# A gated layer's output projection, split by heads between the last group of heads and what follows it

## What is computed

```
def gated_delta_net(h, w_in, conv_w, a_log, dt_bias, norm_w, w_out):
    proj = h @ w_in
    ...
    o = chunk_gated_delta_rule(q, k, v, g, beta)
    o = rms_norm_2(o, norm_w) * jax.nn.silu(z.reshape(B, T, GDN_V_HEADS, GDN_HEAD_DIM))
    return o.reshape(B, T, GDN_V_W) @ w_out
...
        x = x + rms_norm_2(m, norm_mix_post[layer])
        h = rms_norm_2(x, norm_ffn_pre[layer])
        x = x + rms_norm_2(swiglu_2(h, ffn_w_gate[layer], ffn_w_up[layer], ffn_w_down[layer]),
                         norm_ffn_post[layer])
```

## Time and profile before

| | |
|---|---|
| median of 3 runs | 2587.55 us (2573.05 to 2587.69) |
| the profiled execution | span of 2583.7 us from the first to the last instruction |
| TensorE matmul busy, share of that span | 2399.0 us, 93% |
| VectorE, ScalarE, GpSimd | 61%, 45%, 29% |
| mean granted TensorE clock | 0.954 of full |
| the last group of heads, until its last chunk output | from 2222.5 to 2300.9 us |
| the output projection | from 2316.3 to 2364.2 us |

### The profile page before, as it was taken

One profiled execution on the slowest core, in us unless ns is written; L12 is line 12 of the kernel. 1 busy time (PEld: TensorE's weight loads), 2 busy tenths in 40 slices (PEclk: granted clock), 3 DMA queues, 4 the chain that ended last, 5 costly groups with the idle time before them and its releaser, 6 DMA issues. The chain is left out here.

```text
span 2583.7 us, 54823 instructions
## 1 busy us (share of the span) xinstructions
PE 2399.0 (93%) x21962; PEld 2304.5 (89%) x21962; DVE 1588.3 (61%) x2781; ACT 1171.5 (45%) x1907; POOL 739.6 (29%) x653
## 2 busy tenths in 40 slices
PE   7999798999999998999999988989988998879998
PEld 7999687999889998999899987889977888868998
DVE  3779796666524674766566688556675545335665
ACT  3534564443445664434444456444344434524343
POOL 1230496000186554000000078520024454510000
PEclk9999799999999999999999999999998988969999
DMA  4575200555455442555255543245531221203552
GB/s 166 193 200 181 73 1 17 172 185 179 138 174 169 126 136 92 172 185 180 90 187 179 166 140 137 97 142 181 185 116 59 75 79 64 92 2 130 196 185 91
DMA packets 103295, 344.48 MB, mean 133 GB/s; under 512 B 16336, under 2 KB 22000, under 8 KB 102592
## 3 DMA queue, kind: packets, MB, share of 16 engines
q1 hardware_dynamic: 102560, 340.66, 40.1%
q0 software_dynamic: 544, 1.12, 0.3%
HBM read 340.56 MB, written 1.16 MB: 132 GB/s over the span
## 5 line engine op out<-in xcount | busy, mean ns | idle before, releaser
L163 PE MATMUL ps<-h_high,hi 128*128 128x256 f32 x3320 | 977.8, 295 | 48.4 <-DVE h_low L327 29.1
L164 PE MATMUL ps<-h_low,hi 128*128 128x256 f32 x3320 | 954.6, 288 | 0.0
L165 PE MATMUL ps<-h_high,lo 128*128 128x256 f32 x3320 | 953.8, 287 | 0.0
L101 ACT ACTIVATE hi<-raw 128x1024 fp32r<-128x1024 f32 x623 | 648.1, 1052 | 385.2 <-PE ps L165 384.4
L163 PEld LDWEIGHTS ps<-h_high,hi 128*128 128x128 f32 x3320 | 652.0, 196 | 68.2 <-DVE h_low L327 34.2
L123 DVE TENSOR_TENSOR lo<-raw,hi 128x1024 fp32r<-128x1024 f32 x440 | 532.9, 1227 | 231.6 <-ACT hi L101 231.0
L164 PEld LDWEIGHTS ps<-h_low,hi 128*128 128x128 f32 x3320 | 652.8, 197 | 1.3 <-issue 0.6
L165 PEld LDWEIGHTS ps<-h_high,lo 128*128 128x128 f32 x3320 | 652.2, 196 | 0.0
L140 POOL TENSOR_TENSOR lo<-raw,hi 128x512 fp32r<-128x512 f32 x354 | 456.9, 1316 | 316.6 <-ACT hi L101 316.5
L164 PE MATMUL ps<-hidden_low,hi 128*128 128x256 f32 x1056 | 298.7, 283 | 0.0
L163 PE MATMUL ps<-hidden_high,hi 128*128 128x256 f32 x1056 | 296.7, 281 | 1.8 <-DVE lo L123 1.4
(11 more groups left out here) (456 smaller groups left out, 3610.8 us busy)
## 6 DMA issues: line engine op xcount, KB each, us to landing
raw<-in_weights SPq DMA_DIRECT2D x623, 512.0 KB, 3.4
at_bias<-bias_group SPq DMA_DIRECT2D x64, 64.0 KB, 2.7
s_bn<-in_s_bn SPq DMA_DIRECT2D x4, 512.0 KB, 4.7
consts<-in_consts SPq DMA_DIRECT2D x1, 1506.5 KB, 8.8
x<-in_x SPq DMA_DIRECT2D x1, 1024.0 KB, 4.9
s_cT<-in_s_b SPq DMA_DIRECT2D x1, 1024.0 KB, 7.4
s_cw<-in_s_c SPq DMA_DIRECT2D x1, 1024.0 KB, 10.5
s_cT<-s_rows POOLq DMA_DIRECT2D x16, 64.0 KB, 8.0
```

The source lines that it names most:

```text
L101: act.activation(k.hi[:, item % CUT, :], k.raw[:, item % RAW, :], ACT.Copy).then_inc(k.item_rounded, 1)
L163: pe.matmul(out, wh, xh, start=start, stop=False, **more)
L164: pe.matmul(out, wh, xl, start=False, stop=False, **more)
L165: return pe.matmul(out, wl, xh, start=False, stop=stop, **more)
```

## The change

`gdn_out` is dropped and its 128 products move into `gdn_heads`, which now runs with the feed-forward part and the last norm in one Block.

- The 128 products are cut into six parts by heads and columns. Parts 0 and 1 (heads 0 to 7, 64 products) are chained behind the 32 gate products as fill of the last group, which so has 96. Parts 2 and 3 (heads 8 to 11, 32 products) stand around the last group's closing norm: 6 before its sums, 10 between sums and rows, 16 after the rows. Parts 4 and 5 (heads 12 to 15, 32 products) follow.
- Heads 0 to 11 get their high part on ScalarE (`out_high`) and their low part on VectorE (`out_low`) within the last group, two heads after each of levels 1 to 4 and two at two of the chunk steps. GpSimd takes no low parts of heads any more. The pairs lie in the hidden buffers of the feed-forward part, in two new buffers of four tiles, and in the buffers of the layer's input, for which `part_free` waits.
- Columns 0 to 3 of heads 0 to 7 are added up in banks 4 and 5 and copied out (`kept`, two copies of 128 x 512 on VectorE, before its copies of `u`); later VectorE adds them into banks 0 and 1. The results end in banks 0, 1, 4 and 5, and the feed-forward part's gate and up products go to banks 2 and 3.
- All the output projection's weight items are rounded on ScalarE and cut on GpSimd (`cut_halves`); before, VectorE cut them. Weights are stored in the order of the parts.

```
+OUT_PARTS = [(range(0, 8), range(0, 4)), (range(0, 8), range(4, 8)), (range(8, 12), range(4, 8)), (range(8, 12), range(0, 4)),
+             (range(12, 16), range(0, 4)), (range(12, 16), range(4, 8))]
...
+    def part_free(engine, h):
+        if 6 <= h < 14:
+            engine.wait_ge(k.item_used, first + n_proj)
+        elif h >= 14:
+            engine.wait_ge(k.item_used, first + n_proj + 5)
...
+        def out_products(part):
+            heads, cols = OUT_PARTS[part]
...
+            if part == 0:
+                pe.wait_ge(g.read, n_proj)
+            for i, h in enumerate(heads):
+                pe.wait_ge(k.low_done.s, b_low + h + 1)
+                for c, n in enumerate(cols):
+                    if part == 1 and i == 0 and c % 2 == 0:
+                        pe.wait_ge(k.norm_out.s, b_kept + c // 2 + 1)
+                    pair, j = part_of(h)
+                    out = out_at(n + 4) if part == 0 else out_at(n)
...
+                    mm = product(pe, out, w.tile(n_proj * ITEM + at), pair_tile(pair, j), start=opening, stop=last and part in (0, 4, 5),
+                                 skip_group_check=True)
...
+            if hg == NG - 1:
+                fill = itertools.chain(fill, first_out_products())
...
+        fill = more_out_products()
+        some(fill, 6)
         head_sums(NG - 1, iter(()))
+        some(fill, 10)
         head_rows(NG - 1)
+        for _ in fill:
+            pass
+        for part in range(4, 6):
+            for _ in out_products(part):
+                pass
...
             if hg:
                 head_squares(hg - 1)
+            if not more:
+                out_high(0, 2)
             rounded(F, F + 1)
...
-                if more or l < 5:
-                    rounded(F + l - 1, F + l)
+                rounded(F + l - 1, F + l)
                 if hg and l == 4:
                     head_roots(hg - 1)
+                if not more and l < 5:
+                    out_high(2 * l - 2, 2 * l)
...
+                if not more and n in (1, 2):
+                    out_high(6 + 2 * n, 8 + 2 * n)
+                rounded(F + 7 + n, F + 8 + n)
...
         head_squares(NG - 1)
         head_roots(NG - 1)
+        rounded(F + 11, F + 15)
+        out_high(GH - HG, GH)
+        rounded(F + 15, F + 19)
...
+                if not more and l < 5:
+                    out_low(2 * l - 2, 2 * l)
+            if not more:
+                dve.wait_ge(k.item_used, first + n_proj + 4)
+                for b in range(2):
+                    dve.tensor_copy(kept[...], k.ps[:, 4 + b, :]).then_inc(k.norm_out.s, 1)
...
+                elif n in (2, 3):
+                    out_low(4 + 2 * n, 6 + 2 * n)
...
+        out_low(GH - HG, GH)
+        for b in range(2):
...
+            dve.tensor_tensor(k.ps[:, b, :], k.ps[:, b, :], kept[...], ALU.add).then_inc(k.out_done.s, 1)
...
-                if more or l < 6:
-                    cut(F + l - 2, F + l - 1)
+                cut(F + l - 2, F + l - 1)
...
+        cut(F + 9, F + 19)
...
+    k.result_banks, k.gate_banks = (0, 1, 4, 5), (2, 3)
```

More of the change, by code:

```diff
@@ L12 @@
+import itertools
 import math
@@ L417, in norm @@
         return Parts(k, src, pair, kt, gain_col, dst, slot)
[L420 to L457, removed]
 def swiglu(k, src, prep, side=None):
@@ L510, in gate_up @@
                     for j in range(KT):
-                        mm = product(pe, k.ps[:, 4 + b % 2, half * T:(half + 1) * T], w.tile((at + half) * ITEM + j),
+                        mm = product(pe, k.ps[:, gates[b % 2], half * T:(half + 1) * T], w.tile((at + half) * ITEM + j),
                                      pair_tile(src, j), start=(j == 0), stop=(j == KT - 1))
@@ L2545, in gdn_heads @@
     order = gdn_order()
-    first, n_out = k.used, len(order)
+    first, n_proj = k.used, len(order)
+    n_all = n_proj + GH * KT // ITEM
     z = sb("gdn_z", [P, 2 * HG, T])
@@ L2678, in _ @@
         sp.dma_start(par[:, 1, :], k.ins["gdn_dt_bias"].broadcast_to([P, GH])).then_inc(k.side_here.s, 16)
-        loads(k, sp, first, n_out)
+        loads(k, sp, first, n_all)
     @block.tensor
@@ L2723, in head_rows, with first_out_products, more_out_products @@
                     mm.then_inc(g.hw, 1)
+        def out_products(part):
+            heads, cols = OUT_PARTS[part]
+            at = sum(len(a) * len(b) for a, b in OUT_PARTS[:part])
+            if part == 0:
[7 more added lines that the diff above has]
+                    out = out_at(n + 4) if part == 0 else out_at(n)
+                    opening = part in (0, 1, 3) and i == 0 and c % 2 == 0
+                    last = i == len(heads) - 1
+                    mm = product(pe, out, w.tile(n_proj * ITEM + at), pair_tile(pair, j), start=opening, stop=last and part in (0, 4, 5),
+                                 skip_group_check=True)
+                    at += 1
+                    if part >= 4 and last and c == 1:
+                        mm.then_inc(k.result_done.s, 1)
+                    if at % ITEM == 0:
+                        mm.then_inc(k.item_used, 1)
+                    yield
+        def first_out_products():
+            for part in range(2):
+                yield from out_products(part)
+        def more_out_products():
+            for part in range(2, 4):
+                yield from out_products(part)
         prep.sums_before(pe)
@@ L3086, in head_variance, with out_low @@
             ins.then_inc(g.hv, 1)
+        def out_low(a, b):
+            for h in range(a, b):
+                pair, j = part_of(h)
+                dve.wait_ge(k.cut_round.s, b_high + h + 1)
+                dve.tensor_tensor(pair[1][:, j, :], v[:, h, :], pair[0][:, j, :].bitcast(F32), ALU.subtract).then_inc(k.low_done.s, 1)
         def head_inverse(hg):
@@ L3266, in _ @@
                     pool.tensor_tensor(op, op, z_of(hg - 1)[:, 2 * b:2 * b + 2, :], ALU.mult).then_inc(g.ho, 1)
-            if more:
-                cut(F + 5, F + 7)
+            cut(F + 5, F + 7)
             for n in (1, 2):
@@ L3272, in _ @@
                 pool.tensor_tensor(Sd[:, :, :], S[:, n % 2, :, :], spread(rx[:, :, end - 1:end], 2, P), ALU.mult).then_inc(g.sd, 1)
-                if more:
-                    cut(F + 6 + n, F + 7 + n)
+                cut(F + 6 + n, F + 7 + n)
             if more:
                 cut(F + 9, F + 12)
+        cut(F + 9, F + 19)
     A.n += 5
     k.side_here.n += 48
-    k.used += n_out
-    k.late = None
+    k.used += n_all
+    k.late = first + n_all - 1
+    k.result = [(k.out_done.s, b_added + 1), (k.out_done.s, b_added + 2), (k.result_done.s, b_res + 2), (k.item_used, first + n_all)]
+    for signal, n in ((k.mul_done, 2), (k.cut_round, GH), (k.low_done, GH), (k.norm_out, 2), (k.result_done, 2), (k.out_done, 2)):
+        signal.n += n
+    k.result_banks, k.gate_banks = (0, 1, 4, 5), (2, 3)
 def build(nc, ins, x_in, out, plan, n_items):
@@ L3333, in build @@
         k.act_done = counted("scalar_part_done")
-        k.norm_out = counted("norm_tile")
+        k.norm_out = counted("tile_written_by_vector")
         k.cut_round = counted("high_part")
@@ L3537, in gdn_items @@
 def gdn_items(inp):
-    w = inp["gdn_w_in_2"][0]
-    return np.concatenate([by_output(w[:, :6 * D])[gdn_order()], by_output(inp["gdn_w_out_2"][0])])
+    w, out = inp["gdn_w_in_2"][0], tiles(inp["gdn_w_out_2"][0])
+    out = np.concatenate([out[list(heads)][:, list(cols)].reshape(-1, P, P) for heads, cols in OUT_PARTS])
+    return np.concatenate([by_output(w[:, :6 * D])[gdn_order()], as_items(out)])
 def gdn_ba(inp):
```

49 lines of the change are left out of this document (35 added, 14 removed).

## The result

The changed kernel takes 2559.93 us, the median of four runs (2551.97, 2559.49, 2560.37 and 2576.32); the kernel before, with a fourth run added to the three shown ahead, 2583.05. The ratio is 0.9909 with a 95% interval of 0.9884 to 0.9935: faster by 23.1 us, 0.9%. The forecast of 2557.0 is 2.9 us off and the range holds it, but part of that agreement is luck: the saving was put at 30.5 us, 7.4 us too high, and the median of before came out 4.5 us lower than the one it was taken from, which hides most of that.

A forecast was written before the change was run, and what follows sets the result against it. TensorE, 93% busy, bounds the program, and engine-to-engine chains bound the last group and closing norm; 141.75 - 80.9 (group) - 30.3 (behind it) = 30.5 us saved, so 2587.55 - 30.5 = 2557 us, range 2544 to 2573.

The forecast's parts named there:

- The frame: From group 3's first key product to the feed-forward part's first sum of squares: 141.75 us replaced, 30.5 us saved.
- 3.9 us "around the span": Whole run: time of the profiled execution outside its span of 2583.7 us, together the median of 2587.55.
- Group 3 until level 3: Last group's start: TensorE's order unchanged, 24.4 us from the old trace plus 0.8 us.
- The +0.8: Ahead of level 2's copies on ScalarE: two high parts at 0.4 us each, all on the path.
- From level 3 to the end of the group: Group 3 to its last output: group 2's 57.1 us less 1.4 us of square sums.
- VectorE's and ScalarE's additions in the group: Group 3: at most 11.7 us more on VectorE and 13.1 us on ScalarE, costed at nothing.
- Behind the group: Last output to first feed-forward sum: 30.3 us, against 63.3 before.
- The fifth rival: Closing norm's chain as exposed as before: 39.9 us behind the group, 9.6 more, 2567 us; chance 0.04.
- The first, slots without free room: Last group's levels: group 85 to 95 us, 15 to 25 us saved, 2563 to 2573 us; chance 0.24.
- The second, that the clock stays up: Group 3: under 5 us at half clock, some 6 us more back and 2 behind, 2549 us; chance 0.14.
- The third, shared ports: VectorE's low parts and GpSimd's cuts wait for each other: 11 us less saved, 2568 us; chance 0.10.
- The fourth, queues that wait for each other: In-order queues in group and tail: slower than before, 2617 us at 6 us for each place; chance 0.06.

The follow-up runs named there:

- the repetition: The changed kernel run again unaltered, beside the kernel before: median 2563.2 us, ratio 0.9888.
- both edits: Changed kernel with four last-group level 2 products moved into the wait for ScalarE's copies and the last gate read at level 2's end: 2553.12 us, 0.9866 of before.
- the four after it: Both edits plus four products moved in groups 1 and 2 (2545.29, again 2548.54 us), or splits at later levels in group 3 (2551.69) or all groups (2540.68).

## Why the prediction held, and where its steps did not

**The frame.** Right: what follows the stretch takes 219.5 us in every trace, what precedes it differs by the clock of a stage with the same code, and the saving on the stretch (23.0 and 27.7 us) is about that of the medians (23.1 and 25.6). The 3.9 us "around the span" were not that: the changed kernel's profiled execution has 1.8. The rest was the distance between one execution and the median.

**Group 3 until level 3.** The term that was mis-sized is the one that took 24.4 us from the old trace "until level 3", plus 0.8. It measured 29.4 and 28.3 us in the changed kernel, for 25.2. The +0.8 was right in size (0.62 measured). What the term left out is that the old 24.4 us stood at full clock, and that the same order with a longer wait need not. With four products in the wait, level 3 comes at 23.6 to 23.7 us in each of the six traces of group 3 that have them there. Without them and with the wait of 1.9 us it comes at 28.2 to 29.4 in five of six, and at 25.0 in the sixth, the run without products of the output in the group. With the old wait of 1.27 us it comes at 24.4 in both traces. So it is shown that the loss is half clock and that the moved products keep it away; that the 0.62 us of longer wait brought it is possible, and not shown. The trace of before had the warning in it: in groups 1 and 2, which I took as the measured case of "this very order", level 3 comes at 30.9 and 29.7 us. I took the second half from group 2 and the first from group 3's own trace, where it was 5.3 us shorter.

**From level 3 to the end of the group.** 55.7 forecast, 58.2 measured. 1.05 us of that is the wait of the first output product for the last gate result, which the prediction didn't name though the diff shows the wait (`g.read`): shown by moving the read. The other 1.4 us go with the clock: from level 3 on the changed kernel has 14.0 us at half clock, and the piece of group 2 that was the model had 9.5. In the repetition, with 9.8, this part takes 56.4 us.

**VectorE's and ScalarE's additions in the group.** Cost at nothing: nothing speaks against it; no wait for a low part is in the group's list. VectorE was busy there for 34.0 us, forecast at most 36.8.

**Behind the group.** 30.3 forecast, 31.2 measured, with 1.36 us of wait for the squares (1.4). The cover was worth 5.7 us where it could be taken away. The fifth rival, a closing chain as exposed as before, falls.

**The other rivals.** The first, slots without free room, has its size for the group (87.5 us lies in its 85 to 95) and part of its mechanism. The slots are worth 12.9 to 15.7 us of 23.0, so 32 to 44% of the products in them were not free; and its remark that in groups 1 and 2 the half clock falls on other places than in group 3 names what happened. But with the wait filled the group holds all 96 products in 78 us. The second, that the clock stays up, did not come with this change. It needs under 5 us at half clock in the group: the version with both edits has 6.8, and the four after it with more products moved have 3.4 or none, at medians of 2540.7 to 2551.7 us. The third, shared ports, is real in the rows and worth nothing in the time of the tail. The fourth, queues that wait for each other, didn't appear.

**What stays open.** Why one unchanged stage has 20 to 51 us at half clock from one execution to the next; whether it is the idle time amid level 2's tiny matmuls or their order with the large ones that brings the half clock, and why it stayed away in one trace of six; what ends the idle time of groups 1 and 2 there; and whether splitting at every level is better than at one.

## What to carry to other kernels

When a mark of the old trace becomes a term of the sum, look at the granted clock under it and at the same code in its other instances: a half that ran at full clock once is a lower bound. A wait of 1 to 2 us between tiny matmuls can cost more than itself, since the large products behind it may run at half clock, as they did at level 2 in 24 of 30 cases here; four products put into a wait of 1.9 us brought 2.5 us against one trace and 5.3 against another. The slots of this kernel, which looked free, took in 56 to 68% of what was put into them for nothing; count on no more elsewhere until a trace shows it.

## What the hardware showed that I had not expected

The same code took 84.7, 84.9, 85.0 and 87.5 us in four executions of group 3, and one stage far from the change gives 14 us between two traces, through the granted clock. A comparison of two traces end to end would have shown 9.2 us (2583.7 - 2574.5) for a change that is worth 23: compare the stretch between two marks, and what lies before and after it apart.
